# One fused streaming-encoder step: the first quarter of the norm's modulation loaded in two halves, and three more gate blocks begun in the opening

## The reference, cut to what matters

```
def mixer_layer(x, c, pos, past, w_ada, b_ada, ln_gain, w_in, ...):
    mod = jnp.einsum('bd,de->be', jax.nn.silu(c), w_ada) + b_ada
    shift, scale, gate = jnp.split(mod, 3, axis=-1)
    h = rmsnorm(x, ln_gain) * (1 + scale[:, None]) + shift[:, None]
    proj = jnp.einsum('btd,de->bte', h, w_in)
    ...
    q_a, ckv, krope, g_a, q_b, k_b, v_b, q_i, k_i, w_i, g_b = jnp.split(proj, split_at, axis=-1)
    # group A: latent attention over ckv and krope; group B: indexer, top-k, sparse attention
    # the two outputs, normed and gated by silu(g_a), silu(g_b), go through w_out; then x + gate * that
```

## Time and profile before

| | |
|---|---|
| median of three runs | 897.64 us |
| the profiled run, its own time | 897.59 us |
| its span, first to last instruction | 895.8 us |
| TensorE (PE) busy | 870.1 us, 97% |
| VectorE (DVE) busy | 434.3 us, 48% |
| ScalarE (ACT) busy | 334.9 us, 37% |
| GpSimd (POOL) busy | 125.8 us, 14% |
| read from and written to memory | 178.55 MB and 12.69 MB |
| granted TensorE clock, mean | 0.997 |

### The profile page before, as it was taken

One profiled execution on the slowest core, in us unless ns is written; L12 is line 12 of the kernel. 1 busy time (PEld: TensorE's weight loads), 2 busy tenths in 40 slices (PEclk: granted clock), 3 DMA queues, 4 the chain that ended last, 5 costly groups with the idle time before them and its releaser, 6 DMA issues.

```text
span 895.8 us, 13815 instructions
## 1 busy us (share of the span) xinstructions
PE 870.1 (97%) x5580; PEld 764.7 (85%) x5580; DVE 434.3 (48%) x889; ACT 334.9 (37%) x619; POOL 125.8 (14%) x207
## 2 busy tenths in 40 slices
PE   3999999999999999999999999999999999999996
PEld 1577788999999888888999999988999998888886
DVE  3523343336542145443454467364465466677262
ACT  3222352434432334322333353232244436554252
POOL 0000013101200000112340300000312123630000
PEclk9999999999999999999999999999999999999998
DMA  9999958564443253457553567555898833894313
GB/s 370 419 417 417 416 192 253 176 214 161 146 139 116 78 181 107 141 168 243 177 177 96 182 248 258 212 197 198 267 322 276 269 108 112 310 277 138 121 66 122
DMA packets 49919, 190.05 MB, mean 212 GB/s; under 512 B 7584, under 2 KB 8216, under 8 KB 44608
## 3 DMA queue, kind: packets, MB, share of 16 engines
q1 hardware_dynamic: 34848, 141.35, 43.8%
q0 software_dynamic: 14864, 47.30, 16.5%
q10 hardware_dynamic: 144, 0.52, 0.1%
HBM read 178.55 MB, written 12.69 MB: 214 GB/s over the span
## 4 chain that ended last, share of the span: by engine, by line
PE 89%; DMA 4%; DVE 3%; ACT 2%; issue 1%; SPq 0%; DVEq 0%; ACTq 0%
PE proj L1921 34%; PE proj L1910 30%; DMA araw<-in_ada_pairs 4%; PE bankO L1891 3%; PE proj L1942 2%; PE proj L1891 2%; PE bankO L2026 1%; PE bankS L1942 1%; PE bankO L2038 1%; PE bankS L2091 1%; PE bankS L1921 1%; PE bankO L2109 1%; PE bankO L2120 1%; PE bankO L2078 1%; PE bankS L1910 1%
## 5 line engine op out<-in xcount | busy, mean ns | idle before, releaser
L1373 DVE TENSOR_TENSOR w_lo<-raw,w_hi 128x1024 fp32r<-128x1024 f32 (+2 forms) x164 | 196.8, 1205 | 217.3 <-ACT w_hi L1025 216.4
L1025 ACT ACTIVATE w_hi<-raw 128x1024 fp32r<-128x1024 f32 (+2 forms) x164 | 167.8, 1026 | 189.5 <-PE proj L1910 98.5
L1921 PE MATMUL proj<-hT_hi,w_hi 128*128 128x384 f32 x608 | 209.0, 344 | 0.0
L1921 PE MATMUL proj<-hT_hi,w_lo 128*128 128x384 f32 x608 | 203.7, 335 | 0.0
L1921 PE MATMUL proj<-hT_lo,w_hi 128*128 128x384 f32 x608 | 203.5, 335 | 0.0
L1910 PE MATMUL proj<-w_hi,hT_hi 128*128 128x512 f32 (+2 forms) x464 | 176.7, 381 | 0.7 <-DVE hT_lo L1445 0.4
L1910 PE MATMUL proj<-w_hi,hT_lo 128*128 128x512 f32 (+2 forms) x464 | 173.6, 374 | 0.0
L1910 PE MATMUL proj<-w_lo,hT_hi 128*128 128x512 f32 (+2 forms) x464 | 173.4, 374 | 0.0
L1921 PEld LDWEIGHTS proj<-hT_hi,w_hi 128*128 128x128 f32 x608 | 114.2, 188 | 9.1 <-issue 7.5
L1921 PEld LDWEIGHTS proj<-hT_lo,w_hi 128*128 128x128 f32 x608 | 114.2, 188 | 0.1
L1921 PEld LDWEIGHTS proj<-hT_hi,w_lo 128*128 128x128 f32 x608 | 114.1, 188 | 0.0
(11 more groups left out here) (382 smaller groups left out, 1091.8 us busy)
## 6 DMA issues: line engine op xcount, KB each, us to landing
raw<-in_units SPq DMA_DIRECT2D x184, 512.0 KB, 4.1
araw<-in_ada_pairs SPq DMA_DIRECT2D x32, 1024.0 KB, 10.3
wuvT<-in_w_uv_t POOLq DMA_DIRECT2D x8, 512.0 KB, 6.6
...
gate_scratch<-stage POOLq DMA_DIRECT2D x8, 384.0 KB, 3.5
...
```

The lines of the kernel that those rows point to most:

```text
L1025: return nc.scalar.activation(out, in_, func, scale=scale, **kw)
L1373: V.tensor_tensor(w_lo[:, SLOT[u], 0:w], raw_of(u)[:, 0:w], high(u)[:, 0:w].bitcast(F32), ALU.subtract).then_inc(lo_ready, 1)
L1921: ins = mm(banks[blk][:, 0:TOK], w[:, n, cols], a[:, kt, :], start=first and n == m == 0, stop=final and n == per - 1 and m == 2)
```

## The change

1. `ada` 0 (16 units of one k-tile) becomes `ah` 0 and `ah` 1: eight units each, of two k-tiles and half of the quarter's feature columns, with eight matmuls of 128 columns a unit in place of four of 256. Modulation is turned over in five steps (`MODS`) instead of four. The first key unit follows `ah` 0 with an order of its own (`first_unit`): prompt rows first, its halves of w_hi and w_lo made one by one. `ah` 1 comes after it.
2. The transposes are two turns a unit, and the last pair stands behind the key unit. There are six `busy` matmuls instead of seventeen.
3. Gate blocks 1, 2 and 3 are begun in the opening as pieces `gp`, of two or four k-tiles, whose sums are kept in SBUF (`g_kept`); what is left of ga 1, ga 2 and ga 3 is added to these by DVE (line 1912) in place of ACT's copy. ga 2 now ends in the opening; in the middle only ga 3, three units, is left.
4. In the opening the splits are made two plain units ahead. `ql` runs two heads a unit on two banks (`ql`, `qk`).

The steps that follow are placed by row, so those from `osq` to `y` stand one unit later against the blocks around them, and the decode steps lie beside other units.

```diff
 
+ADA = ("ah", "ada")
+MODS = [("ah", 0), ("ah", 1), ("ada", 1), ("ada", 2), ("ada", 3)]
+
+
+PIECES = [(1, (0,)), (2, (0, 0.5)), (3, (0,)), (1, (0.5, 1)), (2, (1, 2))]
+GA_REST = {0: (0, 0.5, 1, 2, 3), 1: (2, 3), 2: (3,), 3: (1, 2, 3)}
+
+
 def chunks():
 
-    out = [("ada", q, 1, 1) for q in range(4)]
-    out += [("kb", 0, 2, NT), ("ga", 0, 4, 2), ("ga", 1, 4, 2), ("ckv", 0, 2, NT), ("m0", 0, 2, NT), ("m1", 0, 2, NT)]
+    out = [("ah", q, 2, 1) for q in range(2)] + [("ada", q, 1, 1) for q in range(1, 4)]
+    out += [("kb", 0, 2, NT), ("ga", 0, 4, 2)] + [("gp", n, 4, 2) for n in range(len(PIECES))]
+    out += [("ga", 1, 4, 2), ("ga", 2, 4, 2), ("ckv", 0, 2, NT), ("m0", 0, 2, NT), ("m1", 0, 2, NT)]
     out += [("qn", j, 4, 2) for j in range(4)]
     out += [("kb", 1, 2, NT)] + [("vb", j, 2, NT) for j in range(2)]
-    out += [("ga", j, 4, 2) for j in range(2, 4)]
...
-    keys, first, second = of("kb", 0), of("ga", 0), of("ga", 1)
-    out = of("ada", 0)
-    for q in range(1, 4):
-        ada = of("ada", q)
-        n = 2 if q == 1 else 4
-        out += ada[:n] + [keys[2 * q - 2]] + ada[n:8] + [first[q - 1]] + ada[8:12] + [keys[2 * q - 1]] + ada[12:]
-        out.append(second[q - 1])
-    out += [keys[6], keys[7], first[3], second[3]]
...
+    a, b = of("ah", 0), of("ah", 1)
+    out = a + key[:1] + b[:2] + g0[:1] + b[2:5] + one + b[5:]
+    b = of("ada", 1)
+    out += two[:1] + b[:4] + key[1:2] + b[4:7] + two[1:] + b[7:10] + g0[1:2] + b[10:13] + three + b[13:]
+    b = of("ada", 2)
+    out += one_b[:1] + b[:4] + key[2:3] + b[4:8] + g0[2:3] + b[8:12] + key[3:4] + b[12:14] + one_b[1:] + b[14:]
+    b = of("ada", 3)
+    out += two_b[:1] + b[:4] + key[4:5] + b[4:7] + g0[3:4] + b[7:10] + key[5:6] + b[10:13] + two_b[1:] + b[13:]
+    out += g1[:1] + key[6:] + g0[4:] + g1[1:] + g2
...
-TURNS = [LAST_UNIT["ada", q] + 1 for q in range(1, 4)]
+LAST_UNIT = {ch[:2]: UNITS.index((c, unit_ks(ch)[-1])) for c, ch in enumerate(CHUNKS)}
+
+
+TURNS = [LAST_UNIT[ch] + 1 for ch in MODS[1:]]
...
-    if u < 0:
-        return 0
-    near = sum(v <= u + LEAD for v in SPLIT_UNITS)
+    if u <= FIRST:
+        return 2 * (u == FIRST)
+    so_far = sum(v <= u for v in SPLIT_UNITS)
     if u in (LAST_UNIT["ada", 3], LAST_UNIT["ada", 3] + 1):
 
         return sum(v <= LAST_UNIT["ada", 3] + 2 for v in SPLIT_UNITS)
     if u < FIRST_UNIT["ckv", 0]:
 
-        return max([near, u > LAST_UNIT["ada", 0]] + [sum(v <= w + AHEAD for v in SPLIT_UNITS) for w in TURNS[:2] if w <= u])
-    return min(max(near, sum(v <= u for v in SPLIT_UNITS) + LEAD - 1), SPLIT_OF[W3_UNITS[LEAD - 1]])
+        return so_far + 2
+    near = sum(v <= u + LEAD for v in SPLIT_UNITS)
+    return min(max(near, so_far + LEAD - 1), SPLIT_OF[W3_UNITS[LEAD - 1]])
...
-    run(1, "xT", 6, 2)
-    run(2, "xS", 6, 2)
-
-    for q in range(4):
-        u = LAST_UNIT["ada", q] + (q > 0)
-        put(u, *([("busy", 2), ("modT", q), ("busy", 4)] if q == 0 else [("modT", q)]))
-        u += q == 0
-        for kind in ("h", "hl"):
-            put(u, (kind, 2 * q), (kind, 2 * q + 1))
-    for n, u in ((1, 13), (2, 14), (1, 16), (6, 17), (1, 18)):
-        put(u, ("busy", n))
+    for n in range(6):
+        put(1 + n + 3 * (n > 4), ("xT", n), ("xS", n))
+
+    for n, ch in enumerate(MODS):
+        u = LAST_UNIT[ch] + (n > 0)
+        if n == 0:
+            put(u, ("w0", 0), ("busy", 1), ("modT", 0), ("busy", 5))
+            put(u + 1, ("h", 0), ("hl", 0), ("w1", 0))
+            continue
+        put(u, ("modT", n))
+        pairs = [1] if n == 1 else [2 * n - 2, 2 * n - 1]
+        put(u, *[(kind, m) for kind in ("h", "hl") for m in pairs])
...
+        def w0(_):
+
+            act.wait_ge(raw_loaded[SLOT[FIRST]], landed[FIRST])
+            copy(high(FIRST)[:, 0:512], raw_of(FIRST)[:, 0:512]).then_inc(hi_ready, 1)
+            copy(high(FIRST)[:, 512:UCOL], raw_of(FIRST)[:, 512:UCOL]).then_inc(hi_ready, 1)
+
         def h(m):
 
             pair = slice(2 * m, 2 * m + 2)
-            act.wait_ge(sem("mod_ready"), m // 2 + 1)
-            emptied(act, "xT", 5)
-            emptied(act, "xS", 5)
+            act.wait_ge(sem("mod_ready"), m + 1 if m < 2 else m // 2 + 2)
+            emptied(act, "xT", 5 if m > 1 else 1)
+            emptied(act, "xS", 5 if m > 1 else 0)
+            if m == 0:
+
+                for kt in range(2):
+                    nc.scalar.activation(hT_hi[:, kt, 0:SEQ], xsT[:, kt, 0:SEQ], ACT.Identity, scale=modT[:, 1, kt, 0:1],
+                                         bias=modT[:, 0, kt, 0:1]).then_inc(sem("hT_hi_ready"), 1)
+                split(SECOND)
+                act.wait_ge(sem("h_ready"), 1)
+                copy(hT_hi[:, pair, SEQ:TOK], xsT[:, pair, SEQ:TOK]).then_inc(sem("hT_hi_ready"), 1)
+                return
             for kt in (2 * m, 2 * m + 1):
...
                                    op1=ALU.mult).then_inc(sem("mod_ready"), 1)
 
+        def w0(_):
+            dve.wait_ge(hi_ready, 1)
+            V.tensor_tensor(w_lo[:, SLOT[FIRST], 0:512], raw_of(FIRST)[:, 0:512], high(FIRST)[:, 0:512].bitcast(F32),
+                            ALU.subtract).then_inc(lo_ready, 1)
+
         def h(m):
 
-            dve.wait_ge(sem("mod_ready"), m // 2 + 1)
-            emptied(dve, "xT", 5)
-            emptied(dve, "xS", 5)
+            dve.wait_ge(sem("mod_ready"), m + 1 if m < 2 else m // 2 + 2)
+            emptied(dve, "xT", 5 if m > 1 else 1)
+            emptied(dve, "xS", 5 if m > 1 else 0)
+            if m == 0:
+
+                for kt in range(2):
+                    ins = V.tensor_scalar(h_first[:, kt, :], xsT[:, kt, 0:SEQ], modT[:, 1, kt, 0:1],
+                                          modT[:, 0, kt, 0:1], ALU.mult, ALU.add)
+                link(ins)
+                for kt in range(2):
+                    if kt:
+                        dve.wait_ge(hi_ready, 2)
+                        V.tensor_tensor(w_lo[:, SLOT[FIRST], 512:UCOL], raw_of(FIRST)[:, 512:UCOL],
+                                        high(FIRST)[:, 512:UCOL].bitcast(F32), ALU.subtract).then_inc(lo_ready, 1)
+                    dve.wait_ge(sem("hT_hi_ready"), kt + 1)
+                    V.tensor_tensor(hT_lo[:, kt, 0:SEQ], h_first[:, kt, :], hT_hi[:, kt, 0:SEQ].bitcast(F32),
+                                    ALU.subtract).then_inc(sem("hT_ready"), 1)
             smp = xsT[:, 2 * m:2 * m + 2, SEQ:TOK].rearrange("p k (b t) -> p k b t", t=DS)
             for a, op in ((1, ALU.mult), (0, ALU.add)):
...
             kind, j = CHUNKS[c][:2]
+            if last_unit(u) and (kind == "gp" and j > 2 or kind == "ga" and j):
+
+                dve.wait_ge(unit_used, u + 1)
+                if kind == "ga":
+                    stored(dve, *staged[staged.index((kind, j)) - 1])
+                kept = g_kept[j if kind == "ga" else PIECES[j][0]]
+                for n, b in enumerate(BANKS[c]):
+                    V.tensor_tensor(stage[:, n, 0:TOK] if kind == "ga" else kept[:, n, :], ps[b][:, 0:TOK], kept[:, n, :],
+                                    ALU.add).then_inc(proj_free[b], 1)
             if last_unit(u) and kind == "gate":
 
                 dve.wait_ge(unit_used, u + 1)
...
+            if u == FIRST:
+                first_unit(hi_, lo_, banks)
+                return
+            if (kind, j) in (("kb", 0), ("ga", 0), ("ga", 1), ("ga", 2)) or kind in ("gp", "wo"):
+
+                pe.wait_ge(sem("hT_ready"), unit_kts(u)[-1] + 1 + MORE + (KT if kind == "wo" else 0))
             if kind in WHOLE:
 
                 pe.wait_ge(raw_loaded[SLOT[own_load(u)]], landed[own_load(u)])
                 clear(0)
-                for g in range(4):
+                for g in range(8 if kind == "ah" else 4):
+                    if kind == "ah":
+
+                        kt, own = 2 * k + g // 4, g % 4
+                        ins = mm(banks[0][32 * own:32 * (own + 1), 0:P], cs[:, kt, :], raw_of(u)[:, P * g:P * (g + 1)],
+                                 start=first and g < 4, stop=final and g >= 4)
+                        continue
...
+                rows = slice(P * t, P * (t + 1))
+                if t == 0:
+                    pe.wait_ge(sem("hT_hi_ready"), n + 1)
+                    pe.wait_ge(hi_ready, n + 1)
+                if t == 2:
+                    pe.wait_ge(sem("hT_hi_ready"), 2 + MORE)
+                mm(banks[t][:], hT_hi[:, n, rows], hi_[:, n, :], start=n == 0, stop=False)
+                if t == 0:
+                    pe.wait_ge(lo_ready, n + 1)
+                mm(banks[t][:], hT_hi[:, n, rows], lo_[:, n, :], start=False, stop=False)
+                if t == 0:
+                    pe.wait_ge(sem("hT_ready"), n + 1)
+                if t == 2:
+                    pe.wait_ge(sem("hT_ready"), 2 + MORE)
+                ins = mm(banks[t][:], hT_lo[:, n, rows], hi_[:, n, :], start=False, stop=False)
             ins.then_inc(unit_used, 1)
 
```

More of the change, by code:

```diff
@@ L77, with unit_ks, unit_kts @@
 CHUNKS = chunks()
+def unit_ks(ch):
+    if ch[0] == "gp":
```

(18 more changed lines are left out.)

182 lines of the change are left out of this document (109 added, 73 removed), and 2 rows, old and new, of the table STEP_BANKS.

## The result

The changed kernel takes 901.95 us (median of 5 runs, 901.32 to 903.66) against 897.64 before (897.52 to 899.76): ratio 1.0043, 95% interval 1.0027 to 1.0059. It is slower by 4.3 us, where +2.5 was forecast. The profiled runs differ by the same amount: span 900.1 against 895.8.

The account below looks back on a forecast made before the run. PE, busy 97% of the span, was taken as the bound. The terms −10.3 + 8.0 − 0.8 + 2.6 + 0.5 + 0.7 + 0.1 + 1.7 sum to +2.5, giving 900.1 us, range 895.3 to 904.0.

Parts of the forecast that it names:

- Start of the projection: Opening: only eight modulation units precede the first key product, which comes at 29.9 instead of 40.27 us; −10.3 us.
- Work behind it: Opening: modulation units, transposes, joins and a modT turn that PE now has behind the first key product; +8.0 us.
- −0.8: Opening: ten or so fillers fewer and the old first quarter's 0.5 us of small load waits gone; −0.8 us.
- The price of 0.53 a unit: Opening: cost in us of each new modulation unit of 16 records, taken as four batches of a filler's 0.133.
- The rival of 58 ns a record: Opening: short modulation records cost 58 ns each, so a new unit takes 0.93 us; about 905.5 us in all; 10%.
- the estimate of about 1.0 a unit: Opening: by the Trainium skill's slow rule all sixteen new modulation units would cost about 1.0 us each; outside the sum.
- Waits on hT_lo: Opening: shorter turn units give less cover, so key units 1 and 2 wait about 0.7 and 1.9 us; +2.6 us.
- the chain modA, modT, h, hT_lo: Opening, where a quarter has ended: steps covered by a turn unit and four modulation units; 6.3 us before PE needs hT_lo.
- Stores: End of the opening: DVE's gate additions wait for stores, delaying the w_lo queued behind; +0.5 us, range 0 to 2.2.
- Decode: Decode steps: the last value unit's three-copy eviction delays ss, +0.7 us; ql's reload has less cover, +0.1 us.
- ysq: RMS sum: a row later, osq waits behind ACT's eviction of the indexer block, so PE waits; +1.7 us (1.2 to 2.0).
- The rival that the waits don't end last: Whole kernel: hT_lo comes earlier, ysq and decode delays are largely hidden; 0.9 left of 5.6 us, 895.4 us; 24%.

Follow-up runs that it names:

- e11: Changed kernel with loads of all modulation pairs behind the fourth halved and splits of the first three turn units one unit later; median 899.31 us.
- e2: Changed kernel with the splits made ahead in the first three turn units (w_hi, w_lo) one unit later; median 900.97 us.
- e7: Changed kernel with key units 1 and 2 two and three modulation units later in the order; median 906.75 us.
- e10: Changed kernel with loads of all modulation pairs behind the fourth cut to half their bytes; median 901.6 us.
- e1: Changed kernel with ysq four units later, behind the gate units, and the y steps behind it; median 900.29 us, ratio to before 1.0028.
- e5: Changed kernel with ysq behind gate units, turn units' splits one unit later, output banks exchanged, last value block evicted behind decode steps; median 902.31 us.
- e9: Changed kernel with ysq behind gate units, turn units' splits one unit later, output blocks' banks exchanged; median 898.76 us, ratio to before 1.0004.

## Why the prediction came out as it did

The direction was right, and so were the mechanisms of the waits that it named; the size was 1.8 us short. By its own terms:

- *Start of the projection, −10.3*: 29.9 forecast, 30.04 measured; the unit's end gained 10.0. Right to 0.3. The wait on hT_hi (0.81) lies inside it.
- *Work behind it, +8.0, and −0.8*: at the bias product, −10.0 and the new waits of 2.5 and 0.85 leave 7.5 of the measured +0.8; the terms say 7.2. The −0.8 was counted twice: but for two records of fillers at 44.44, 0.3 us, all the fillers that went and the load waits of before (0.84 and 0.30) lie ahead of 40.27, inside the first term. So the +8.0 measured 7.8. The price of 0.53 a unit was a little high: the eight units took 4.0 (0.58, 0.57, 1.44 and 1.45), not 4.2. The rival of 58 ns a record falls: 48 records in 1.44 us are 30 ns each. With it falls the estimate of about 1.0 a unit, which takes for each record the 62 ns that the Trainium skill ("TensorE: Matmul & The Clock Gate", section "Wait — 56ns, not 53.3ns?") gives for a matmul decoded in microcode. Counted by matmuls of the program, which leave two records each, the same rows give 60 ns, so on that count the page's figure is not refuted.
- *Waits on hT_lo, +2.6*: 0.97 and 1.50, 2.5 in all, against 0.7 and 1.9 (the third wait, 0.16, is one of before). Right in sum. e11 shows that they are the chain's, e2 and e7 that little would be won by curing them.
- *modT, not forecast*: 0.85. The step that failed is the cover of "the chain modA, modT, h, hT_lo": the prediction asked when a half-size turn unit has PE want hT_lo, and not when it has PE want the bank that modT is read from. e10 keeps 0.38 of the wait, which is that part. The other 0.47 is the load of the w_lo in front of modT, which in after lands at 69.3; in the turn of before from which the chain was priced it had landed.
- *Stores, +0.5*: 0.3, with the store landing 3.2 us behind its issue. Inside its range, but PE shows no wait there, and runs with the same opening differ by as much in this stretch.
- *Decode, +0.7 and +0.1*: 0.7 at the fifth scores, and 0.2 at the eighth, which was not foreseen there; the reload of w_uk cost nothing that shows.
- *ysq, +1.7*: 1.95, of which 1.5 are the wait. e1 gives it back.
- *The output block's banks, not forecast*: +0.4. Gate block 2 now has fixed banks, so every later pair changes places and the last gate B block has the pair that the output block wants at once. It is in the diff, in the function that deals out the banks, and the prediction did not follow that function to the kernel's end.

The rival that the waits don't end last is wrong: each was there, and five edits that took waits away show what each was worth. But its cousin is true in the opening: there a wait taken away came back in part as a wait on a load (in e2 2.8 us went and 1.08 came). The earlier trace rows held the warning, a DMA share of 0.98 beside a busy PE: two limits that stood level.

What was there to be won is easily misread. Of the 10.0 us that the first key unit gained, 7.5 went to more work behind it: some 6 that used to stand ahead of it, and the joins of the shorter units. Only 2.5 could be kept. Without any loss the bias product would have stood 2.5 ahead of 144.54, where the kernel before has it with the same work ahead. e11 has it at 142.28, with light loads and the chain out of the way; with full loads e2, e5 and e9 have it at 144.75, 144.68 and 144.15.
